# A two-layer decoder step on one core: logits on four column quarters, sums cleared by ScalarE, three modulation units in other waits

## What is computed

```python
for layer in range(2):
    shift, scale, gate = ada_mod(c, w_ada[layer, 0], b_ada[layer, 0])   # silu(c) @ w + b, 1024 -> 3072
    h = x * (1 + scale) + shift
    m = mixer_even(h, ...) if layer == 0 else mixer_odd(h, ...)
    x = layer_norm(ALPHA * x + (1 + gate) * m, ln_g[layer, 0], ln_b[layer, 0])
    shift, scale, gate = ada_mod(c, w_ada[layer, 1], b_ada[layer, 1])
    h = x * (1 + scale) + shift
    m = hier_moe(h, ...)
    x = layer_norm(ALPHA * x + (1 + gate) * m, ln_g[layer, 1], ln_b[layer, 1])

def hier_moe(h, ...):                     # 4 groups of 4 experts, 512 hidden channels each
    pc = softmax(t @ w_coarse + b_coarse) # 4 coarse logits: the best group
    fine = t @ w_fine + b_fine            # 16 fine logits: the two best experts of that group
    out = sum over the token's two experts of  weight * (silu(t @ w_gate) * (t @ w_up)) @ w_down
```

## Time and profile before

| what | us |
|---|---|
| median of 3 runs (796.13 to 798.38) | 797.68 |
| profiled execution, its own time | 798.2 |
| its span in the trace | 796.4 |
| attention and convolution, norms, projection of layer 0 | 120 to 205 |
| routing of layer 0 | 211 to 234 |
| expert loop of layer 0 | 234 to 460 |
| routing of layer 1 | 539 to 559 |
| expert loop of layer 1 | 559 to 778 |

### The profile page before, as it was taken

One profiled execution on the slowest core, in us unless ns is written; L12 is line 12 of the kernel. 1 busy time (PEld: TensorE's weight loads), 2 busy tenths in 40 slices (PEclk: granted clock), 3 DMA queues, 4 the chain that ended last, 5 costly groups with the idle time before them and its releaser, 6 DMA issues.

```text
span 796.4 us, 22089 instructions
## 1 busy us (share of the span) xinstructions
PE 709.8 (89%) x9481; PEld 461.0 (58%) x9481; DVE 280.5 (35%) x681; ACT 226.3 (28%) x404; POOL 120.4 (15%) x213
## 2 busy tenths in 40 slices
PE   3999999899899999877777988989999999979682
PEld 1578877577465565544444656755656565645351
DVE  1138998841751212110110266138121212112017
ACT  1135667520432222211111244025122222212111
POOL 0021587710011111000000000001110101001000
PEclk9999998899999999989898999999999999989897
DMA  9998953599994999999999999999899999999941
GB/s 310 391 341 240 328 202 106 175 365 335 357 402 193 365 417 422 416 416 420 419 416 418 408 381 388 405 408 405 304 420 420 417 417 422 416 416 422 416 191 55
DMA packets 78907, 282.00 MB, mean 354 GB/s; under 512 B 13694, under 2 KB 14148, under 8 KB 66535
## 3 DMA queue, kind: packets, MB, share of 16 engines
q1 hardware_dynamic: 76562, 274.05, 87.7%
q0 software_dynamic: 1600, 5.70, 2.3%
q10 hardware_dynamic: 676, 1.24, 0.5%
HBM read 278.54 MB, written 3.37 MB: 354 GB/s over the span
## 4 chain that ended last, share of the span: by engine, by line
PE 63%; DMA 19%; DVE 9%; SPq 5%; ACT 3%; issue 2%; DVEq 0%; ACTq 0%
PE bank L799 17%; DMA arena<-in_w_up 13%; PE bank L1079 7%; PE bank L808 7%; PE bank L778 6%; PE bank L837 5%; PE bank L642 5%; PE bank L941 5%; DMA arena<-in_w_gate 3%; DMA arena<-in_w_ada 3%; DVE t L1432 3%; SPq L502 2%; DVE arena L1426 1%; PE bank L661 1%; PE bank L828 1%
## 5 line engine op out<-in xcount | busy, mean ns | idle before, releaser
L799 PE MATMUL bank<-arena 128*32 128x256 f32 x3136 | 195.5, 405 | 40.0 <-DMA arena<-in_w_up 30.0
L799 PEld LDWEIGHTS bank<-arena 128*32 128x32 f32 x3136 | 113.3, 117 | 115.2 <-issue 60.5
L1879 DVE SCALAR_TENSOR_TENSOR arena<-arena,bank 128x128 f32<-128x128 f32 x49 | 17.0, 347 | 309.1 <-ACT arena L1374 309.1
L808 PE MATMUL bank<-arena 128*32 128x256 f32 x1568 | 93.6, 379 | 0.0
L2006 POOL TENSOR_TENSOR arena<-t 128x192 f32<-128x192 f32 x51 | 26.5, 520 | 382.2 <-PE bank L778 382.1
L778 PE MATMUL bank<-htm,arena 128*32 128x256 f32 x1224 | 75.8, 379 | 0.0
L1377 ACT ACTIVATE arena<-bank 128x256 f32<-128x256 f32 x49 | 18.9, 385 | 199.7 <-PE bank L808 199.7
L941 PE MATMUL bank<-arena 128*128 128x264 f32 x320 | 73.9, 389 | 1.4 <-ACT arena L1218 1.4
L941 PEld LDWEIGHTS bank<-arena 128*128 128x128 f32 x320 | 59.9, 190 | 13.1 <-ACT arena L1218 1.6
L1374 ACT ACT_TABLE_LOAD x49 | 62.9, 1283 | 1.7 <-issue 0.8
L808 PEld LDWEIGHTS bank<-arena 128*32 128x32 f32 x1568 | 47.5, 110 | 25.2
(11 more groups left out here) (260 smaller groups left out, 638.8 us busy)
## 6 DMA issues: line engine op xcount, KB each, us to landing
arena<-in_w_down SPq DMA_DIRECT2D x32, 2048.0 KB, 25.5
arena<-in_w_ada SPq DMA_DIRECT2D x24, 2048.0 KB, 19.0
arena<-in_w_gate SPq DMA_DIRECT2D x22, 2048.0 KB, 26.3
arena<-in_w_up SPq DMA_DIRECT2D x44, 1024.0 KB, 23.3
arena<-in_w_up SPq DMA_DIRECT2D x10, 2048.0 KB, 20.7
arena<-in_w_gate SPq DMA_DIRECT2D x20, 1024.0 KB, 20.4
arena<-in_w_in_even SPq DMA_DIRECT2D x5, 2048.0 KB, 23.0
arena<-in_w_out_even SPq DMA_DIRECT2D x2, 2048.0 KB, 11.5
```

What stands on the lines that cost most here:

```text
L799: last = mm(GU[C * q:C * (q + 1), :].rearrange("p (a j i) -> p a j i", a=2, j=KF), hgc[:, C * k:C * (k + 1)], cols, start=(k == 0), stop=( ...
L808: last = mm(Y[C * dq:C * (dq + 1), :], hidt[:, C * q:C * (q + 1)], wd[:, q, 2 * P * dq:2 * P * (dq + 1)], start=(q == 0), stop=(q == 3), t ...
```

## The change

Seven edits:

1. The eight logits products write to four quarters of the bank's partitions, tiles 0 and 4 to the first, 1 and 5 to the second, and so on. The transposition becomes a product with a matrix of four stacked identities (`K_FOLD`, 20 columns more in the constants), which also adds the quarters. The bias tile `br` grows to 128 partitions and is zeroed first.
2. `clear_sums` is gone. ScalarE copies zeros into banks 3 to 5 behind its copies of `htm`, ahead of its copies of the units; into bank 2 behind these; into `SAMPLES` when VectorE has copied the tables. TensorE waits for the last before the loop.
3. Unit 5's products move behind the spread product of the convolution's mean, its copy behind the second copy of partial sums.
4. The column products of unit 11 move from behind unit 12 to behind the logits; those of unit 12 stay behind unit 13, where they were.
5. VectorE's eight scalings of `x` (layers' second norm input, `scale_x`) are cut into four pairs: at once, behind the sample logits, behind the picks and behind the tables.
6. The three warm products ahead of layer 1's expert loop are dropped.
7. `TURNED` (7 for each layer) replaces `2 * TT` (6) in the counts of `tm_a`, since ScalarE now signals once more.

```diff
@@ TensorE, routing
+                def part(dst, k, tokens):
+                    q = C * (k % 4)
+                    return mm(dst[q:q + 20, :], wr[:, l, k, :], h[:, k, tokens], start=(k < 4), stop=(k >= 4),
+                              tile_position=(0, q))
...
-                            last = mm(LOGITS_S[l], wr[:, l, i, :], h[:, i, SEQ:T], start=(i == 0), stop=(i == KD - 1))
+                            last = part(LOGITS_S[l], i, slice(SEQ, T))
...
-                    last = mm(LOGITS[l][:, 0:SEQ], wr[:, l, k, :], h[:, k, 0:SEQ], start=(k == 0), stop=(k == KD - 1))
+                    last = part(LOGITS[l], k, slice(0, SEQ))
                 last.then_inc(E("route_logits"), 1)
+                if l == 0:
+                    ada_columns()
                 pe.wait_ge(E("route_lg"), 2 * l + 2)
                 for t in range(TT):
-                    last = tr(ROUTE[:, 20 * t:20 * t + 20], lgt[:, P * t:P * (t + 1)], ident[0:20, 0:20])
+                    last = mm(ROUTE[:, 20 * t:20 * t + 20], lgt[:, P * t:P * (t + 1)], con[:, K_FOLD:K_FOLD + 20],
+                              start=True, stop=True)
@@ TensorE, moe
                 pe.wait_ge(E("logits_zeroed"), l + 1)
-                clear_sums(2, 4, 5)
                 pe.wait_ge(m["table_ready"], l + 1)
...
                 gather(1)
                 tables()
-                clear_sums(3)
-                pe.wait_ge(m["tabs_copied"], l + 1)
-                clear_sums(6)
+                pe.wait_ge(E("tm_a"), TURNED * (l + 1))
@@ TensorE, order of work
             last.then_inc(E("attention_step"), 1)
-            ada_unit(5, False)
...
             mm(bank[3][:, 0:T], ones, ln_part[:, :], start=True, stop=True).then_inc(E("norm_sums"), 1)
+            ada_unit(5, False)
             pe.wait_ge(E("norm_sq"), 1)
...
-            ada_unit(12)
+            ada_unit(12, False)
...
-            keep_warm(3, 6)
             moe(1)
@@ ScalarE
                 copy(t1[:, r:4:2, SEQ:T], bank[2 + r][:, 0:2 * NS].rearrange("p (a t) -> p a t", a=2), E("os_copied"))
-            ada_unit(5)
...
             copy(ln_part[:, :], bank[4][:, 0:T], E("cn_part_copied"))
+            ada_unit(5)
...
                 token_major(l, htm, 2)
+                nothing = lambda n: ysb.unsqueeze(1).broadcast_to([P, n, 2 * P])
+                act.wait_ge(E("tm_a"), TURNED * l + 2 * TT)
+                A(fn(banks[:, 3:6, :].rearrange("p b (a n) -> p (b a) n", a=2), nothing(6), ACT.Copy))
                 for i in units:
                     ada_unit(i)
+                A.sync()
+                A(fn(bank[2].rearrange("p (a n) -> p a n", a=2), nothing(2), ACT.Copy))
+                act.wait_ge(M[l]["tabs_copied"], l + 1)
+                A(fn(SAMPLES, ysb[:, 0:DK], ACT.Copy), E("tm_a"))
@@ VectorE
-                if idx == 1:
-                    return
-                for k in range(KD):
+                if idx != 1:
+                    scale_x(idx, 0)
+            def scale_x(idx, k0):
+                for k in range(k0, k0 + 2):
                     ts(x[:, k, :], t1[:, k, :], ln_scaled[:, 0, KD * idx + k:KD * idx + k + 1],
...
                 one_op(lgt[:, SEQ:T], LOGITS_S[l], br[:, l:l + 1], ALU.add, E("route_lg"))
+                scale_x(2 * l, 2)
...
                 tt(num, num, e2, ALU.mult)
+                scale_x(2 * l, 4)
                 dve.wait_ge(E("route_ranks"), l + 1)
...
                     [P, 2, TT, NCH]), ALU.mult, M[l]["hots_ready"])
+                scale_x(2 * l, 6)
                 ada_copy(*((2, 0), (3, 4))[l])
```

More of the change, by code:

```diff
@@ L75 @@
 K_NONE = K_HEAD + 7
-K_ALL = K_NONE + EXPERTS
+K_FOLD = K_NONE + EXPERTS
+K_ALL = K_FOLD + 20
 NSLOT = 10
@@ L148, in shape_constants @@
     k[NS:, K_NONE:K_NONE + EXPERTS] = -NONE
+    for n in range(20):
+        k[n::C, K_FOLD + n] = 1.0
     return k
@@ L194, in build @@
         wr = sb("wr", [P, 2, KD, 20])
-        br = sb("br", [20, 2])
-        lgt = con[0:20, K_MASK + D:K_MASK + D + TT * P]
+        br = sb("br", [P, 2])
+        lgt = con[:, K_MASK + D:K_MASK + D + TT * P]
         ln_part = sb("ln_part", [P, T])
@@ L334, in build @@
         MEAN_PART, VAR_PART = ([bank[i][:, 0:T] for i in n] for n in ((5, 0, 1, 0), (0, 4, 4, 4)))
-        LOGITS, LOGITS_S = [bank[i][0:20, 0:SEQ] for i in (0, 4)], [bank[i][0:20, 0:NS] for i in (1, 5)]
+        LOGITS, LOGITS_S = [bank[i][:, 0:SEQ] for i in (0, 4)], [bank[i][:, 0:NS] for i in (1, 5)]
+        TURNED = 2 * TT + 1
         ACT_TILES = 6
@@ L537, in _ @@
                 if name == ("ada", 5):
+                    sp.wait_ge(dve_n, 1)
                     for l in range(2):
@@ L759, in ranks @@
                 pe.wait_ge(E("route_mask"), l + 1)
-                pe.wait_ge(E("tm_a"), 2 * TT * l + 1)
+                pe.wait_ge(E("tm_a"), TURNED * l + 1)
                 flat = mask4.rearrange("p t n -> p (t n)")
@@ L811, in down @@
                     last.then_inc(m["down_done"], 1)
[L813 to L818, removed]
                 def rows_ready(n):
@@ L837, in scatter @@
                             last = mm(SUM[2 * dq + b], ysb[r, P * b:P * (b + 1)], sct[r, 0:SEQ], start=False, stop=final and b == 1,
-                                      tile_position=(C * dq, 0))
+                                      tile_position=(C * dq, 0), skip_group_check=True)
                     return last
-                pe.wait_ge(E("tm_a"), 2 * TT * (l + 1))
+                pe.wait_ge(E("tm_a"), TURNED * l + 2 * TT)
                 pe.wait_ge(E("logits_zeroed"), l + 1)
-                clear_sums(2, 4, 5)
                 pe.wait_ge(m["table_ready"], l + 1)
@@ L1161, in _ @@
             ranks(1)
-            pe.wait_ge(E("tm_a"), 2 * TT + 3)
+            pe.wait_ge(E("tm_a"), TURNED + 3)
             ada_unit(23)
             ada_columns()
-            keep_warm(3, 6)
             moe(1)
@@ L1352, in token_major @@
                 for hf in range(2):
-                    act.wait_ge(E("tm_tr"), 6 * use + 2 * t + hf + 1)
+                    act.wait_ge(E("tm_tr"), 2 * TT * use + 2 * t + hf + 1)
                     copy(dst[0:n, t, :].rearrange("p (k m i) -> p m k i", k=KD, m=KD)[:, 4 * hf:4 * (hf + 1)],
@@ L1435, in one_op @@
                 return S(v.tensor_scalar(out, a, s1, None, op), signal)
+            S(v.memset(br[:, :], 0.0))
             S(v.memset(htm[:, 2, :], 0.0), E("htm_zeroed"))
```

2 lines of the change are left out of this document (1 added, 1 removed).

## The result

The changed kernel took 800.91 us (median of 11 runs, 798.66 to 803.19); the kernel before, measured beside it, took 798.12 us (11 runs, 796.13 to 799.76). The ratio is 1.0033, with a 95% interval of 1.0019 to 1.0047: slower by 0.3%, where 795.2 us (793.4 to 797.4) was forecast. The profiled execution took 802.39 us, with a span of 800.53 against 796.38.

A forecast was written before the change was run, and what follows sets the result against it. TensorE's chain and waits for weight matrices alternate as limits in the loops. Gains of 0.95 + 1.35 + 0.2 = 2.5 us take the profiled 798.2 to 795.7 us; from the median 795.2, range 793.4 to 797.4.

The forecast's parts named there:

- Term B: Routing of layer 0 (212 to 234 us): 1.35 us gained, bounds 0.8 to 2.0.
- The three clearing products: Layer 0, ahead of the gather: 0.81 us of products drop out, 0.15 us of the bounds load stays bare.
- Unit 13 starts at 223.55: Layer 0: unit 13 follows unit 12's copy, which waits behind ScalarE's clear; 0.8 us gained, not 1.85.
- the clear's price: Layer 0: ScalarE's clear of 1536 columns in banks 3 to 5 takes 1.5 us, at 1 ns a column.
- Rival 3: Second loop: without warm products the clock falls, first chunk's products cost up to 3.0 us more; about no change; 10%.
- Rival 4: Both routings: ScalarE's clear much dearer than its columns; no faster from 3.1 us, 800.2 us at 4.4; 8%.
- Term A: Unit 5 moved, around 155 us: projection's first tile ends earlier, unit 6 at full clock; 0.95 us gained.
- The logits: Layer 0: logits products on four quarters run side by side and end at 215.5; gain 1.25 to 1.3 us.
- Term C: Routing of layer 1 (539 to 559 us): 0.9 us gained at the gather, mostly given back on VectorE; 0.2 us.
- One to one: Ahead of an expert loop, TensorE's gain moves the release of weight transfers and all behind it by as much.

The follow-up runs named there:

- e3: Kernel before with the sums cleared by ScalarE and nothing else changed; 799.70 us, ratio 1.0017.
- e9: Changed kernel with the clears put back on TensorE, everything else kept; 796.05 us, ratio 0.9975.
- e10: Changed kernel itself, unchanged, timed and profiled again; 799.02 us, ratio 1.0027 against the kernel before.
- e4: Kernel before with only unit 5 moved; 797.54 us, ratio 1.0001.
- e5: Kernel before with logits on quarters, unit 11's columns behind them, late scalings and unit 5 moved; clears on TensorE and warm products kept; 795.57 us, ratio 0.9974.
- e12: Changed kernel with ScalarE's 1536-column clear placed behind its copies of the units; 797.46 us, ratio 1.0002 against the kernel before.
- e11: Changed kernel with two unused products behind the ranks in each layer and layer 1's three warm products put back; 797.71 us, ratio 0.9999 against the kernel before.
- e1: Changed kernel with two unused products put ahead of unit 13 in layer 0; 798.50 us, ratio 1.0006 against the kernel before.

## Why the prediction was wrong, by its own steps

**Term B failed, at two steps.** "The three clearing products (0.81 us, ending at 230.45) drop out ahead of the gather ... I take 0.15": the load of the bounds, bare, shows as 0.47 us of idle time in e3, near the upper bound of 0.5 (a bound that came from no row), and the drop is worth 0.1 us instead of 0.65. "Unit 13 starts at 223.55, before 224.37: 0.8 us gained": the clear's price was right, yet 0.5 was gained (11.15 us against 11.66), since ScalarE gets to unit 12's copy 1.0 us earlier, not 1.3 (in e9 at 221.34, 9.17 us behind the first logit, against 10.16): the turned logits, now products with 128 rows, take 0.84 us instead of 0.36. The same table shows what I did not weigh: with the clears on TensorE unit 13 gains 1.34 us (e9). I had the clear's delay as a smaller gain, and never asked whether the clear as such was worth it: it gives 0.1 us and takes 0.8 at unit 13 and 0.2 at the first chunk. So at full clock layer 0 would have gained some 0.5 us (e10's 22.23 less the 1.6 of the fall, against 21.10) where I had 1.35.

**The clock in layer 0 was not in the sum at all.** I had left a row of 1.00 as it was, although the change put an idle wait between two units. It costs 1.6 and 2.8 us in the two profiles, and turns the term's sign. Rival 3 had the mechanism, but at the second loop only, with the dropped warm products as its cause, and at 10%.

**Rival 4**, the only one on the slower side, had the right culprit for the wrong reason: the clear is not dear (1.46 us, where 3.1 was the point that decides). Its position on ScalarE is.

**Term A held.** The copy of the sums at 153.0 (forecast 153.7), unit 5 at half clock until 158.3 (158.7), unit 6 at full clock (1.94), the projection waiting for ScalarE at 164.94 (164.6): 0.67 us gained where 0.95 stood. One execution can't say more: over nine profiles with unit 5 moved the way from the input projection's first product to the output projection's took 127.78 us on average (127.03 to 128.56), over five without 128.93 (127.43 to 130.03). Alone its gain is below what the times resolve (e4).

**The logits held**: 3.28 us from the first logit to the turned ones instead of 4.65, 1.37 for a forecast of 1.3. **Term C held in outline and came to nothing**: the gather 0.6 us earlier (0.9 forecast), since GpSimd's selection came 0.3 us earlier behind the first logit and not 0.6, given back by the late scalings on VectorE and the hand-over; 0.02 us lost where 0.2 gained stood. By e9, 0.2 of it is the clears'. **One to one held too**: from the end of the first loop to the second's logits 80.74 to 80.81 us passed in every profile, and the earlier start stayed.

What the prediction had right shows when the failing part is left out. e9 is the changed kernel but for the clears: its ratio of 0.9975 is 2.0 us, where the sum forecast 2.5. e5, equal to it, has the lowest median here, 795.57 us.

**What stays open.** Medians of e10 and e9 lie 2.97 us apart, and by their ratios 4. Their profiles give 1.0 for the waits in layer 0, 1.6 for the clock, and 0.2 in layer 1: 2.8, nearly the former and not the latter. e12, with no fall in its profile, is still 1.4 us above e9 by medians, and its two routings account for 0.5 of that; the rest stands in no row that I have. The changed kernel's first set of runs (800.91) is 1.9 us above its second (799.02), and I can't divide that between the circumstances of a set and falls of the clock, since only one execution of each set has a trace. How often the clock falls in an execution is likewise only known by the four of nine. That e11 and e12 are faster than e10 (by 1.3 and 1.6 us) lies just within the spread of twelve runs each; the rows, not these times, carry the mechanism.

## What to carry to other kernels

Before work is moved off the busiest engine, ask what it covers there and what it will stand in front of at its new place: the clearing products hid a register load of 0.5 us, and at its new place the wide clear stood ahead of a copy for which another engine's next product was waiting. If the work must move, put it behind whatever others wait for (e12), not ahead of it. An edit that opens even 0.4 to 0.75 us of idle time on TensorE in a sparse stage should carry the price of a half-clock stretch times its chance, wherever the profile before shows 1.00; a second profile of the same kernel can show that such a stretch wanders, as it did here.

## What the runs showed of the hardware that was not expected

- The same program falls to half clock at different places: unit 14 of layer 0 took 3.64 us in one execution and 1.94 in another, unit 13 2.67 and 3.54. With that place mended (e1), a fall stood at the twin place of the other layer. "TensorE: Matmul & The Clock Gate" of the Trainium skill, section "What's actually happening", has the throttled state as the default from which activity releases; these rows agree in that each fall came behind the ranks' small products and 0.41 to 0.76 us of idle time; but as much of both (0.41 to 0.86 us idle) lay in five routings without a fall. In the three routings with two warm products in that place there was none.
- ScalarE writes to PSUM at the price of SBUF: 1536 columns took 1.46 us and 512 took 0.60, so 0.84 ns a column and 0.17 us besides; that line gives 1.06 us for 1056 columns, and the SBUF row took 1.07. "ScalarE: Activation LUTs", section "Step-by-step: what each stage is for", of the Trainium skill calls the write to PSUM faster; for these widths the trace shows no difference, and the measurement decides.
- A product with 20 columns and 128 rows of 32-bit data took longer in threes than the transposition it replaced: 0.84 us for three, where the transpositions took 0.36. The trace has six records for the three products and three for the transpositions, so it is 0.14 and 0.12 us a record.
